# A second modulation turn on GpSimd in the rkv stage, and five TensorE pieces fewer in the scan

## The reference, cut to what matters

```python
c_act = jax.nn.silu(c)                        # 2048 values
mod = c_act @ w_ada[l] + b_ada[l]             # w_ada: 2048 x 12288, 100 MB
sh1, sc1, gt1, sh2, sc2, gt2 = jnp.split(mod[:, None, :], 6, axis=-1)
h = _rmsnorm(x, norm1_g[l]) * (1.0 + sc1) + sh1
p = h @ w_in[l]                               # r, k, v, low-rank parts, pool part
y_rwkv = _rwkv7_mixer(p[..., :N_RWKV_COLS], ...)   # the scan
y_pool = _pool_mixer(p[..., N_RWKV_COLS:], ...)
mix = jnp.concatenate([y_rwkv, y_pool], -1) @ w_out[l]
x = x + gt1 * mix
h = _rmsnorm(x, norm2_g[l]) * (1.0 + sc2) + sh2
x = x + gt2 * _conv_ffn(h, w_up[l], conv_w[l], conv_b[l], w_down[l])
```

## Time and profile before

| | |
|---|---|
| median of three runs | 2655.5 us |
| profiled execution | 2664.16 us |
| its span | 2662.3 us |
| mean granted TensorE clock | 0.978 |
| TensorE matmul busy | 2578.9 us (97%) |
| VectorE busy | 1877.7 us (71%) |
| ScalarE busy | 1097.0 us (41%) |
| GpSimd busy | 413.3 us (16%) |
| DMA, mean | 214 GB/s |

### The profile page before, as it was taken

How to read it: one execution, slowest core, us unless ns; L and a number is a source line. 1 busy time by engine, 2 the same in 40 slices (tenths; PEclk the granted TensorE clock), 3 DMA queues, 4 the chain that set the end, 5 groups by cost and what they waited for, 6 DMA issues and landing times.

```text
span 2662.3 us, 41991 instructions
## 1 busy us (share of the span) xinstructions
PE 2578.9 (97%) x18000; PEld 2238.7 (84%) x18000; DVE 1877.7 (71%) x2469; ACT 1097.0 (41%) x1312; POOL 413.3 (16%) x272
## 2 busy tenths in 40 slices
PE   6899999999999999999999999999999999999997
PEld 3678877788888888888889999999888888889996
DVE  2238753277999999999987777776547875886554
ACT  2253322244433443434455544444434444444453
POOL 0047111021000000000020677760000000000001
PEclk8899999799999999999999999999999999999998
DMA  9958477876898888888955887875766656666663
GB/s 341 340 168 229 124 242 246 260 201 179 233 273 260 262 259 261 253 267 253 269 177 133 225 214 219 224 202 175 190 194 178 168 165 189 175 159 174 190 187 114
DMA packets 744921, 570.21 MB, mean 214 GB/s; under 512 B 44544, under 2 KB 629376, under 8 KB 744608
## 3 DMA queue, kind: packets, MB, share of 16 engines
q1 hardware_dynamic: 744736, 567.52, 73.2%
HBM read 565.38 MB, written 2.10 MB: 213 GB/s over the span
## 4 chain that ended last, share of the span: by engine, by line
PE 78%; DVE 13%; DMA 4%; issue 2%; ACT 2%; POOL 1%; SPq 0%; DVEq 0%; POOLq 0%
PE bank L865 28%; PE bank L868 14%; PE bank L832 4%; DVE w_low L1951 4%; PE bank L833 3%; PE bank L834 3%; PE bank L1118 2%; PE bank L821 2%; PE bank L1270 2%; PE bank L1271 2%; PE bank L1272 2%; DMA ring<-w_up 2%; PE bank L903 2%; PE bank L902 2%; PE bank L901 2%
## 5 line engine op out<-in xcount | busy, mean ns | idle before, releaser
L1951 DVE TENSOR_TENSOR w_low<-ring,w_high 128x2048 fp32r<-128x2048 f32 (+1 forms) x389 | 891.6, 2294 | 331.0 <-ACT w_high L1489 324.5
L865 PE MATMUL bank<-acts,w_high 128*128 128x512 f32 x4128 | 993.4, 393 | 1.6 <-ACT vd L1902 1.6
L1489 ACT ACTIVATE w_high<-ring 128x2048 fp32r<-128x2048 f32 (+1 forms) x389 | 738.7, 1901 | 429.3 <-DMA ring<-w_up 186.4
L865 PEld LDWEIGHTS bank<-acts,w_high 128*128 128x128 f32 x4128 | 759.9, 189 | 152.4 <-issue 2.8
L868 PEld LDWEIGHTS bank<-acts,w_low 128*128 128x128 f32 x4128 | 529.2, 191 | 21.0 <-DVE w_low L1951 1.0
L868 PE MATMUL bank<-acts,w_low 128*128 128x256 f32 x4128 | 535.6, 283 | 0.5 <-DVE w_low L1951 0.5
L769 POOL TENSOR_SCALAR prod_g<-adg,cact 128x512 f32<-128x512 f32 x60 | 121.6, 2027 | 64.4 <-DMA adg<-w_ada 61.1
L1270 PE MATMUL bank<-w_high,hid_high 128*128 128x512 f32 x320 | 125.2, 391 | 2.9 <-DVE w_low L1951 2.9
L1271 PE MATMUL bank<-w_low,hid_high 128*128 128x512 f32 x320 | 124.7, 390 | 0.0
L1272 PE MATMUL bank<-w_high,hid_low 128*128 128x512 f32 x320 | 124.5, 389 | 0.0
L691 POOL TENSOR_TENSOR sumf<-sqf 128x256 f32<-128x256 f32 x1 | 0.7, 742 | 781.2 <-ACT sqf L1932 781.2
(11 more groups left out here) (470 smaller groups left out, 3512.8 us busy)
## 6 DMA issues: line engine op xcount, KB each, us to landing
ring<-w_in SPq DMA_DIRECT2D x176, 1024.0 KB, 5.8
ring<-w_up SPq DMA_DIRECT2D x88, 1024.0 KB, 8.2
ada<-w_ada SPq DMA_DIRECT2D x76, 1024.0 KB, 6.8
adf<-w_ada SPq DMA_DIRECT2D x48, 1024.0 KB, 5.2
ring<-w_down SPq DMA_DIRECT2D x44, 1024.0 KB, 6.8
ring<-w_out SPq DMA_DIRECT2D x16, 1024.0 KB, 5.9
adg<-w_ada SPq DMA_DIRECT2D x64, 256.0 KB, 5.5
ring<-w_mla SPq DMA_DIRECT2D x16, 1024.0 KB, 5.7
```

What stands on the lines that cost most here:

```text
L865: pe.matmul(o, wh[:, j], both, start=j == 0, stop=False, skip_group_check=True)
L1489: act.activation(WH[s][:, 0:WIDE[n]], ring[s][:, 0:WIDE[n]], ACT.Copy).then_inc(high_done, 1)
L1951: v.tensor_tensor(WL[s][:, 0:WIDE[n]], ring[s][:, 0:WIDE[n]], f32(WH[s][:, 0:WIDE[n]]), ALU.subtract)\
```

## The change

GpSimd's list of turns in the rkv stage grows from turn 19 to turns 18 and 19, with an accumulator for each; TensorE's turns drop from 19 to 18, so ten instead of eleven stand in the scan and behind it. Five `mod_piece` calls are left out: at levels 1 and 2 of the second half the one between the two groups of blocks, and in the second, third and fourth chunk the one between S/Y and U. SP's `first_turns` goes on over units 17, 18, 20, 21 and 23 and three more behind the last unit. The one `ada` call sums both accumulators, and VectorE takes eight columns instead of four. The load of `xT` back into its place comes one turn earlier in SP's queue.

```diff
+def level_pieces(tt, lv):
+    return 1 if tt == 1 and lv in (1, 2) else 2
-        acc_e = at("acc_e", 8, [P, 512])
+        acc_e = [at(f"acc_e{k}", 8 + 2 * k, [P, 512]) for k in range(2)]
-        N_EARLY, N_FIRST, N_TURNS, N_FFN, N_LATE = 8 + 11, 1, 12, 11, 4
-        FIRST_TURNS = ((0, 16 + 3),)
+        N_EARLY, N_FIRST, N_TURNS, N_FFN, N_LATE = 8 + 10, 2, 12, 11, 4
+        FIRST_TURNS = ((0, 18), (0, 19))
...
-                elif k in (8, 9, 11, 12, 14, 15):
+                elif k in (8, 9, 11, 12, 14, 15, 17, 18, 20, 21, 23):
                     first_turns(1)
+            first_turns(3)
...
                         if eighth == j == 0:
-                            ins = pool.tensor_scalar(acc_e[:, :], w, col, None, ALU.mult)
+                            ins = pool.tensor_scalar(acc_e[t][:, :], w, col, None, ALU.mult)
                         else:
                             after(pool.tensor_scalar(prod_e[:, :], w, col, None, ALU.mult))
-                            ins = pool.tensor_tensor(acc_e[:, :], prod_e[:, :], acc_e[:, :], ALU.add)
+                            ins = pool.tensor_tensor(acc_e[t][:, :], prod_e[:, :], acc_e[t][:, :], ALU.add)
...  (TensorE, between the two groups of blocks of a level)
-                    mod_piece()
+                    if level_pieces(tt, lv) == 2:
+                        mod_piece()
...  (TensorE, chunk n, between S/Y and U)
-                    mod_piece()
+                    if n == 0:
+                        mod_piece()
...
-                        ada(acc_e)
+                        ada(*acc_e)
...  (ScalarE)
-                for n in LEVELS[1:]:
+                for lv, n in enumerate(LEVELS[1:]):
-                    mod_piece(2)
+                    mod_piece(level_pieces(tt, lv))
-                    mod_piece(2)
+                    mod_piece(2 if n == 0 else 1)
...  (VectorE)
-                        v.tensor_copy(mod[:, 76:80], bank[6][:, 0:4]).then_inc(ada_free, 1)
+                        v.tensor_copy(mod[:, 72:80], bank[6][:, 0:8]).then_inc(ada_free, 1)
```

## The result

The changed kernel takes 2664.04 us (median of nine runs, 2661.47 to 2669.43) against 2656.36 of the kernel before: ratio 1.0033, 95% interval [1.0021, 1.0045], which is +8.8 us (the two medians differ by 7.7). A second series of twelve runs gave 2663.78 us and 1.003 [1.0021, 1.004]. Forecast were 2661.9 us, +6.4.

What follows compares the result with a forecast made beforehand. VectorE was taken to be last on the keys and at the end of the rkv stage, TensorE to bound the scan. +5.3 + 6 - 4.9 = +6.4 us on 2655.5 gave 2661.9 us, range 2650 to 2671.

Steps and rivals of the forecast that it cites:

- The reading: In the rkv stage VectorE is last on the keys and at the end; in the scan TensorE is busy 113.36 of 114 us.
- The keys: Rkv stage: GpSimd's second turn slows VectorE's iterations 13 and 14, part of 15; +5.3 us, bounds +2 and +7.2.
- The end of the stage: Rkv stage, VectorE's 21.3 us from unit 20 to `AR` under eighths 4 to 7: +6 us, between nothing and 10.2.
- The whole stage: Rkv stage: the steps on the keys, +5.3 us, and on the end of the stage, +6, taken together.
- The scan: Five pieces out give -5.9 us, four more column matmuls in `ada` cost +1.0: -4.9, bounds -3 and -6.
- wrong by 296: Sign for the keys: `token_sums` near 299.4 us if right; the step is wrong if it starts by 296.
- the 24 of its sign: Sign for the end of the stage: wrong if VectorE's stretch from unit 20 to `AR` stays under 24 us.
- the 3 to 6 of its sign: Sign for the scan: wrong if M24 to `w_out` shortens by less than 3 us or more than 6.
- the clock rival: Third chunk keeps 2.4 GHz, -5.5 us: 2656.4; decides where the rkv stage loses less than 10.4 us; chance 0.19.
- The light case: GpSimd's eighths miss VectorE's dense stretches: +2 and +3, less 4.9, 2655.6 us; chance 0.12.
- the heavy one: VectorE is hit as on the keys throughout: 7.2 + 10.2 - 4.9 = +12.5, 2668.0 us; chance 0.17.
- the lock: Rkv stage: the shared port is an exclusive lock for GpSimd's multiplies too, +29.7 us, 2685.2; chance 0.02.

Runs made afterwards that it cites:

- the last half: Changed kernel with the arithmetic of eighths 1 to 3 of GpSimd's second turn left out, eighths 0 and 4 to 7 made; 1.0014 of the kernel before.
- the turn alone: Against the kernel before, GpSimd makes the second turn but its result is not used, and no piece is taken out; 1.0055.
- the pieces alone: Changed kernel with the five pieces out but GpSimd making only one turn, turn 18 left out; 0.9982 of the kernel before.
- the second profile of before: The kernel before with no edit, profiled once more; 2649.36 us in its profiled execution.

## Why the prediction was right

**The reading.** VectorE behind TensorE on the keys and again at the end of the stage, the scan bound by TensorE, and therefore a loss larger than the gain: all three hold, in the profile after and in the experiments that take each away.

**The keys: +5.3 forecast, 3.8 to 4.7 measured** (K in the three profiles with the whole turn among the keys). The mechanism is as told, the two iterations are not: 5.4, 7.7 and 6.9 us for iterations 13, 14, 15 of after instead of 7.4, 7.4 and 5.5. The first multiply of the turn began at 276.22, under VectorE's `w_low`, and gave way (3.56 us), so the first iteration stayed nearly free, and the eighths were closer together than forecast, so the third was hit. Fetching the tiles was timed well: first use 276.2 (277 forecast), eighth 4 at 325.5 (326), end 358 (356).

**The end of the stage: +6 forecast.** The stretch E grew by 4.2 us, to the tenth in every kernel with the last half. M24 gave up to 2 us of it back (A is 2.3 where it was 3.6 to 4.5), because the piece ahead of it no longer waits for its tile; the prediction saw that wait go and gave it no gain. But the count stopped at `AR`, and VectorE went on: the identities, copies of 0.43 us, took up to 1.49 us, and `Kt`, which the transposes wait for, came 4 to 5 us later after M24. So this step measures 4.2 - 2 + 5 = 7 us, not 6: nearly the right size, for partly wrong reasons.

**The whole stage: +11.3 forecast, 13.5 measured** in time (14.6 with the turn alone). Unit 1 to M35 takes 162.2 to 165.8 us without the second turn, 176.4 to 177.9 with it, +14 between the means. K and the end make some 11 of these. The other 2.4 us lie in the stretch between them, from `token_sums` to the scaled keys, to which the prediction gave nothing: 27.8 to 31.1 us, 28.9 on the average, in the eight profiles without the second turn's arithmetic in the stage, and 29.8 to 32.4, 31.3 on the average, in the six with half or all of it. It goes with the clock: `token_sums` takes 3.77 to 6.11 us in the eight and 4.89 to 6.96 in the six. The two ranges overlap, so it is likely but not shown that the turn does it. By size this is the whole miss, +6.4 forecast and +8.8 measured.

**The scan: -4.9 forecast, -4.8 measured** with the pieces alone, and that they agree is partly luck. In the profiles the scan is 187.9, 181.0 and 180.4 us with the pieces and 174.3 to 178.3 in the seven with five of them out, -7 between the means. The terms were off both ways: the third chunk's piece was priced at 1.67 us from a low clock that the second profile of before doesn't have, and `ada` with eight columns took 1.92 us where the clock held and 2.04 to 3.14 where it fell, 2.87 in after, for 1.02 before. A wait also appeared, though not at the places of the pieces. Where the fourth chunk keeps the full clock, TensorE waits 3.3 to 5.0 us behind the scan for VectorE's `hn`; that is so in five of the seven, and the wait is 0.3 to 1.0 us in the other nine profiles. In the kernel with the pieces alone:

```profile
520.18 6.49 PE L1020 MATMUL bank<-con,hn 128*64 128x128 f32 x64 [4.98 <-DVE hn L2291]
```

**The signs.** `token_sums` came at 297.3 us (near 299.4 forecast, wrong by 296), M24 at 353.8 (near 357), `w_out` at 545.5, 1.9 us behind before where 6 were forecast. VectorE's stretch from unit 20 to the end of `AR` is 25.8 us, over the 24 of its sign. M24 to `w_out` shortened by 5.5 us, inside the 3 to 6 of its sign, but only because T, which grew by 4, lies in it: M35 to `w_out` shortened by 9.5 in this pair of profiles, and much of that is the low clock of the first profile of before.

**The rivals.** The third chunk keeps the full clock in the profile of after, as the clock rival had it (1.00 where before showed 0.50):

```profile
492.00:504.00 12.00, 12.00 (x294) 9.28 (x290) 1.53 (x3) 2.98 (x5) 0.00 (x0) 1.00 0.67 221
```

But this is no effect of the change: the third chunk keeps it in the second profile of before and in the one of the turn only as well, both with all pieces in. The 0.50 of the earlier trace rows belongs to one execution, and a gain of 5.5 us could not be read from it. Nor was it decisive: the 10.4 us of loss in the rkv stage, its point of decision, were exceeded. The light case is refuted by K and E, the heavy one by E at 4.2 of 10.2.

As for the lock: in after one multiply of 1.6 us stretched to 3.56 under `w_low`, so VectorE does hold off GpSimd's multiply, while multiplies still held off VectorE's two-input instructions by tenths. The rule of the Trainium skill (SBUF — State Buffer, "Who interferes with whom") holds here with GpSimd's add first and with VectorE first. With GpSimd's multiply first it does not: in after `w_low` starts at 289.16, inside the multiply of 288.11 to 289.73, and takes its usual 2.29 us. That section also counts VectorE's copies among the instructions that can contend, and the trace agrees: the identity copy at 353.68 took 1.49 us, to just behind the end of the GpSimd add of 352.24 to 354.89.

## What to carry to other kernels

Before work is moved to an idle engine, look at what it shares with the engine that is nearly full: here 58 us of work on GpSimd made the kernel 13.5 us longer, most of it at two places where TensorE waits for VectorE, and the five matmul pieces bought 5. Follow the slowed engine past the instruction that you first find on the path, to the end of its dense stretch. And compare profiles by marks in a stage, on two executions of the same kernel first: K and E repeat to 0.1 us in the two profiles of before, whose spans differ by 15, and E also in the two of the changed kernel, where K differs by 0.9. A clock that one profile shows in one chunk is no property of the kernel.

## What the runs showed that was not expected

The kernel before itself varies by 17 us over its runs (2648.69 to 2665.36), and between its two profiles by 14.7 us of span. 6.9 us of that lie in the scan and 2.3 in `token_sums` (6.11 and 3.77 us), with the same code and about 3 us of waits in the scan in both. TensorE's granted clock there was at its lower level of 1.2 GHz for a longer time in the first. A difference of 8.8 us between two kernels can vanish in one pair of profiles, as it did here.

GpSimd's adds beside VectorE are slowed as well: 1.27 us in the scan, where VectorE has little to do, up to 3.31 in the rkv stage of after.
